# Retention of a two-layer hybrid block: a chunked recurrence in place of the full quadratic form

## The chip, the cores and the metric

The kernel runs on one core of a Trainium2 chip. The metric is the device time of one execution in microseconds. The core has five engines with queues of their own that meet only at semaphores: TensorE (PE), VectorE (DVE), ScalarE (ACT), GpSimd (POOL) and SyncE (SP), which starts the DMA transfers. All data are fp32; the large projections are done in three passes over high and low parts (fp32r).

## The reference

512 latent tokens x and 256 context tokens h, width 1024, pass through two layers. Each layer: a modulated RMSNorm, one input projection to 2304 columns, three head groups (retention, windowed attention, gMLP gating), an output projection, then a SwiGLU FFN. The change is in retention (4 heads of 64):

```python
def retention_scan(q, k, v, log_gamma, s0):          # CHUNK = 128
    ...
    intra = jnp.where(diff >= 0, jnp.exp(lg[:, :, None] * jnp.maximum(diff, 0.0)), 0.0)
    ...
    def step(s, inp):
        qi, ki, vi = inp
        sc = jnp.einsum('bhqd,bhkd->bhqk', qi, ki) * intra
        o = jnp.einsum('bhqk,bhkv->bhqv', sc, vi) + jnp.einsum('bhqd,bhdv->bhqv', qi * q_decay, s)
        s = s * chunk_decay + jnp.einsum('bhkd,bhkv->bhdv', ki * k_decay, vi)
        return s, o
```

It runs forwards and backwards, first over the context from a zero state, then over the latent tokens from the final states of the context. The two outputs are summed, normalised per head and gated:

```python
    o_f, st_f = retention_scan(q, k, v, lg_f, s0_f)
    o_b, st_b = retention_scan(q[:, :, ::-1], k[:, :, ::-1], v[:, :, ::-1], lg_b, s0_b)
    o = (o_f + o_b[:, :, ::-1]).transpose(0, 2, 1, 3)
```

Layer 1 needs no outputs for the context, only its keys and values.

## The kernel before, in words

Activations lie transposed: features on the 128 partitions, tokens along the rows (columns 0 to 511 latent, 512 to 767 context; NT = 768, SX = 512, SC = 256). Chunks 0 to 3 are latent, 4 and 5 context. Every engine has one program written out by hand, in order; a wait holds up all that is behind it on its engine.

A layer runs through these stages:

- Norm, then nine input panels (`in_step`) of two halves. PE does the three passes (L1284 to L1286). ACT makes the high part of the next weights (`hi_a`, L474) and evicts the result; POOL makes the low part (`lo_a`, L379); DVE applies rotary embedding (L965 to L968) to the keys, queries and attention operands. In layer 0, PE also computes the modulation vectors beside the panels: `mod_half` (L1224), whose row DVE copies out (`mod_copy`, L805), and `mod_finish` (L1232), for which PE waits on that copy after the first half of the next panel. At the end of panel 1 in layer 0 DVE computes the logs of the decays (`log_decay_b`, L851 to L865), ahead of the `mod_copy` of that panel.
- gMLP: after the last panel, 48 (layer 0) or 32 (layer 1) small matmul records (L1354).
- Retention, full quadratic form. For each head h and key chunk c there is a job: `score` (L1370) multiplies the 64 features of 128 keys with all 512 queries; DVE multiplies the result with the decay table T or TC (L1038) into Pm; `value` (L1382) multiplies with the values and accumulates over the chunks. There are 24 jobs in each layer, and 8 of 256 columns for context queries in layer 0. PE runs two scores ahead. The tables of a head are made by DVE (L985, L986, L1017, L1018) and ACT (`tables`, L620 to L625). The context's contribution comes through TC, a sum of both directions, without states. The gMLP gates (`gate`, L1002 to L1009) are spread between the jobs on DVE. ACT copies the output to osb (`copy_out`), and PE's attention waits for both halves of it.
- In the same stretch ACT and POOL make the high and low parts of the attention keys and queries (akh, akl, aqh, aql; ACT L474, POOL L436 and L379). Attention waits for the last (qk_lo, 6).
- Attention: scores (L1434 to L1436), softmax (DVE L1092, ACT L704), transposes (L1452), values (L1460), with the group norm of retention in between (L1402, L1408). Then output projection, norm, FFN.

At the start SP loads, in this order: c, constants up to the masks, x, context, five modulation panels, small tensors, three more panels, then the other constants (masks, distances, rotary tables) and the first weights.

Of the kernel before, what the change touches and what calls it, by code (L numbers as in the profile page):

```python
# [21 lines left out]
P = 128  # L22
# [3 lines left out]
SX = 512  # L26
# [30 lines left out]

class Chain:
# [19 lines left out]
def trunk(nc, x, c, ctx_in, c_ctx, w_mod, b_mod, norm1_g, norm2_g, w_in, ret_decay_f, ret_decay_b, ret_norm_g,  # L78
          attn_sink, cm_norm_g, cm_w_s, cm_b_s, w_out, w_gate, w_up, w_down, final_norm_g, consts, out):
    stack = ExitStack()  # L80
    with stack:
# [10 lines left out]
        def overlay(specs, under=()):  # L92
# [10 lines left out]
        K = sb("consts_sb", [P, K_ALL])  # L103
        xT = sb("xT", [P, KC, NT])
        zh = sb("zh", [P, KC, NT], F32R)
# [17 lines left out]
        blg = sb("blg", [P, 16])  # L123
# [3 lines left out]
        eye = K[:, K_EYE:K_EYE + P]  # L127
        ones = K[:, K_ONES:K_ONES + P]
        blk = K[:, K_BLK:K_BLK + P]
        dist = K[:, K_DIST:K_DIST + DIST_W]  # L130
        ropeC = K[:, K_RC:K_RC + SX]
        ropeS = K[:, K_RS:K_RS + SX]
# [28 lines left out]
        T, TC, TD, osb, Pm = overlay([  # L161
            ("T", [P, 2, DIST_W], F32), ("TC", [P, 2, 640], F32), ("TD", [P, 640], F32), ("osb", [P, 2, NT], F32),
            ("Pm", [P, 3, SX], F32)],
            under=[(n + "_r", s, d) for n, s, d in mix_base])

        gn = Pm[:, :, :].rearrange("p a n -> p (a n)").rearrange("p (a n) -> p a n", a=2)
        oc, gsq = gn[:, 0, :], gn[:, 1, :]
# [54 lines left out]
        def _(sp):  # L222
# [7 lines left out]
            sp.dma_start(K[:, 0:K_MASK], consts[:, 0:K_MASK]).then_inc(sem("ld_x"), 16)  # L230
# [24 lines left out]
            sp.dma_start(K[:, K_MASK:K_ALL], consts[:, K_MASK:K_ALL]).then_inc(sem("ld_tables"), 16)  # L255
# [119 lines left out]
        def _(pool):  # L375
# [45 lines left out]
            for l in range(DEPTH):  # L421
# [7 lines left out]

                pool.wait_ge(sem("loA"), 2 * A_OUT[l] + 2)  # L430
# [39 lines left out]
        def _(act):  # L470
# [77 lines left out]
            for l in range(DEPTH):  # L548
# [31 lines left out]
                for p, name in enumerate(PANELS):  # L580
                    for h in range(2):
# [35 lines left out]
                def tables(h):  # L617
                    act.wait_ge(sem(f"T_arg{l}"), h + 1)
                    i, b = l * 4 + h, h % 2
                    nc.scalar.activation(T[:, b, :], T[:, b, :], ACT.Exp)  # L620
                    nc.scalar.activation(TC[:, b, :], dist[:, 0:640], ACT.Exp, bias=blg[:, i:i + 1], scale=lg[:, i:i + 1])
                    if h:

                        act.wait_ge(sem(f"T_done{l}"), h)
                    nc.scalar.activation(TD[:, :], dist[:, 0:640], ACT.Exp, bias=blg[:, 8 + i:9 + i],  # L625
                                         scale=nlg[:, 8 + i:9 + i]).then_inc(sem(f"T_exp{l}"), 1)

                if l == 0:
                    act.wait_ge(sem("ld_tables"), 16)
                tables(0)  # L630
                def copy_out(r):

                    act.wait_ge(sem(f"ret_pv{l}"), (r + 1) * (16 if l == 0 else 12))
                    if l == 0:
                        copy(osb[:, r, SX:NT], ps[:, 6, 0:SC])
                    copy(osb[:, r, 0:SX], ps[:, 5, :]).then_inc(sem(f"osb_rdy{l}"), 1)

                tables(1)
                e = 0
                for c0, c1, s in parts(l == 0):  # L640
                    for r in range(2):
                        act.wait_ge(sem(f"cm_f{l}"), e + 1)
                        copy(zh[:, 6 + r, c0:c1], cmf[:, e % 2, 0:c1 - c0]).then_inc(sem(f"cm_hi{l}"), 1)
                        e += 1
# [153 lines left out]
        def _(dve):  # L798
# [50 lines left out]
            def log_decay_b():  # L849
# [14 lines left out]
                ch.link(V.tensor_scalar(blg[:, 0:8], lg[:, 0:8], float(SX), None, ALU.mult))  # L864
                ch.link(V.tensor_scalar(blg[:, 8:16], lg[:, 8:16], float(SC), None, ALU.mult))  # L865
# [61 lines left out]
            for l in range(DEPTH):  # L927
# [28 lines left out]
                if l == 0:  # L956
                    dve.wait_ge(sem("ld_tables"), 16)
                rope_n = 0
                for p, name in enumerate(PANELS):
                    for h in range(2):  # L960
# [10 lines left out]
                        if l == 0 and p == 1 and h == 1:  # L971
                            log_decay_b()
# [10 lines left out]
                def table(h):  # L983
                    i, b = l * 4 + h, h % 2
                    ch.link(V.tensor_scalar(T[:, b, :], dist, lg[:, i:i + 1], None, ALU.mult))  # L985
                    V.scalar_tensor_tensor(T[:, b, :], dist, nlg[:, 8 + i:9 + i], T[:, b, :], ALU.mult, ALU.min  # L986
                                           ).then_inc(sem(f"T_arg{l}"), 1)

                dve.wait_ge(sem("cm_mm"), l + 1)
                table(0)  # L990
                cm_jobs = [(r, c0, c1, s) for c0, c1, s in parts(l == 0) for r in range(2)]

                def gate(e):

                    if e < len(cm_jobs):
                        r, c0, c1, s = cm_jobs[e]
# [621 lines left out]
```

## Time and profile before

| | |
|---|---|
| median of 3 runs | 2117.64 us (2115.95 to 2118.99) |
| the profiled execution: its own time | 2115.09 us |
| its span, first to last instruction | 2113.3 us |
| mean granted TensorE clock | 0.899 |
| PE, DVE, ACT, POOL busy | 88%, 37%, 25%, 26% |
| retention stage, layer 0 | 279.18 to 394.64 us |
| retention stage, layer 1 | 1421.74 to 1517.91 us |

The page of the profile gives busy times of the engines, the span in 40 slices with the granted clock (PEclk, in tenths of full speed), the chain that ended last, and groups of instructions. A group's row has line, engine, operation, output<-inputs, shapes and count, then busy time and mean ns of one, then the idle time in front and who ended it. A line of the timeline has start, duration, engine, line and operation; "x6" stands for six instructions merged, and the bracket tells how long the engine had been idle and what released it. An fp32 matmul leaves two MATMUL records and two weight loads (PEld); the records of a transpose and of fp32r matmuls are single.

### The profile page before, as it was taken

To read this page: it belongs to the slowest core of one execution; us is meant where nothing else is said; L and a number is where in the kernel's file an instruction comes from. 1 tells how busy PE (TensorE), PEld (TensorE's weight loads), DVE (VectorE), ACT (ScalarE), POOL (GpSimd) and SP (SyncE) were. 2 spreads that over 40 slices of the span, in tenths; PEclk is the share of its full clock that TensorE was granted. 3 is DMA by queue.
4 is the path that set the end of the run, shared out by engine and by line. 5 is a ranking of instruction groups with operands and counts; after the bars stand their busy time and mean duration, and the time that the engine had idled before them with its cause. 6 is when DMAs were issued, how large, how long until landed. Compare 5 with 4: busy or idle time off the path is not lost.

```text
span 2113.3 us, 21910 instructions
## 1 busy us (share of the span) xinstructions
PE 1869.8 (88%) x8746; PEld 1369.4 (65%) x8746; DVE 786.3 (37%) x1194; ACT 537.9 (25%) x850; POOL 550.5 (26%) x244
## 2 busy tenths in 40 slices
PE   4799989787877999999999978879978869999997
PEld 2577732354665888888888867761344647787875
DVE  3331442355245222222222274245253352433335
ACT  3212230245322211111111122332144232222222
POOL 1522211000133322222222213333000344434430
PEclk8799965789987999999999988995689979999999
DMA  6444400000041333332222101230000313132321
GB/s 243 166 139 142 137 20 0 0 1 1 20 139 44 116 100 100 99 99 99 99 99 99 40 21 36 64 80 0 0 1 1 95 44 120 60 119 67 112 79 41
DMA packets 121900, 155.53 MB, mean 74 GB/s; under 512 B 20320, under 2 KB 89712, under 8 KB 121712
## 3 DMA queue, kind: packets, MB, share of 16 engines
q1 hardware_dynamic: 121840, 154.71, 22.7%
q8 instruction: 40, 0.66, 0.1%
q14 instruction: 20, 0.16, 0.0%
HBM read 152.60 MB, written 2.10 MB: 73 GB/s over the span
## 4 chain that ended last, share of the span: by engine, by line
PE 63%; issue 16%; DVE 10%; ACT 5%; POOL 3%; DMA 2%; SPq 1%; POOLq 0%; DVEq 0%; ACTq 0%
PE ps L1284 13%; PE ps L1285 12%; PE ps L1286 12%; PE ps L1510 5%; PE ps L1511 4%; PE ps L1512 4%; PE ps L1382 3%; PE ps L1370 3%; POOL wl L379 2%; PE ps L1224 2%; DVE nxz L920 2%; PE ps L1460 1%; ACT s_at L704 1%; DVE nxz L914 1%; DVE hl L1163 1%
## 5 line engine op out<-in xcount | busy, mean ns | idle before, releaser
L1284 PE MATMUL ps<-zh,wh 128*128 128x512 f32 x1728 | 631.4, 365 | 77.0 <-DVE zl L905 38.1
L379 POOL TENSOR_TENSOR wl<-raw,wh 128x1024 fp32r<-128x1024 f32 x144 | 354.3, 2472 | 1186.2 <-ACT wh L474 1186.2
L1285 PE MATMUL ps<-zl,wh 128*128 128x512 f32 x1728 | 623.4, 361 | 0.0
L1286 PE MATMUL ps<-zh,wl 128*128 128x512 f32 x1728 | 619.5, 359 | 0.0
L1284 PEld LDWEIGHTS ps<-zh,wh 128*128 128x128 f32 x1728 | 333.9, 193 | 173.1 <-issue 70.4
L1286 PEld LDWEIGHTS ps<-zh,wl 128*128 128x128 f32 x1728 | 333.5, 193 | 49.6
L1285 PEld LDWEIGHTS ps<-zl,wh 128*128 128x128 f32 x1728 | 334.7, 194 | 45.6
L474 ACT ACTIVATE wh<-raw 128x1024 fp32r<-128x1024 f32 x144 | 148.5, 1058 | 409.7 <-PE ps L1286 206.4
L1176 DVE SCALAR_TENSOR_TENSOR xT<-ps,modcol,xT 128x512 f32<-128x512 f32 (+1 forms) x264 | 169.3, 661 | 103.2 <-PE ps L1512 99.2
L1157 DVE TENSOR_TENSOR hf<-gs,ps 128x512 f32<-128x512 f32 x66 | 37.5, 596 | 414.3 <-ACT gs L748 414.3
L1510 PE MATMUL ps<-hh,wh_d 128*128 128x512 f32 x480 | 173.1, 361 | 12.2 <-DVE xT L1176 12.2
L1511 PE MATMUL ps<-hl,wh_d 128*128 128x512 f32 x480 | 171.5, 357 | 0.0
L1512 PE MATMUL ps<-hh,wl_d 128*128 128x512 f32 x480 | 170.8, 356 | 0.0
L748 ACT ACTIVATE gs<-ps 128x512 f32<-128x512 f32 x44 | 26.3, 597 | 461.8 <-PE ps L1286 461.8
L379 POOL TENSOR_TENSOR wl_d<-raw_d,wh_d 128x1024 fp32r<-128x1024 f32 x40 | 95.0, 2397 | 174.1 <-ACT wh_d L474 174.1
L1382 PE MATMUL ps<-Pm,vtok 128*64 128x512 f32 (+1 forms) x112 | 102.2, 1023 | 12.3 <-DVE Pm L1038 12.3
L1163 DVE TENSOR_TENSOR hl<-hf,hh 128x768 fp32r<-128x768 f32 (+1 forms) x44 | 76.6, 1742 | 95.3 <-ACT hh L474 95.3
L1510 PEld LDWEIGHTS ps<-hh,wh_d 128*128 128x128 f32 x480 | 91.2, 190 | 30.0 <-DVE xT L1176 16.5
L1370 PE MATMUL ps<-rq,rk 64*128 64x512 f32 (+1 forms) x112 | 102.5, 1020 | 0.0
L1512 PEld LDWEIGHTS ps<-hh,wl_d 128*128 128x128 f32 x480 | 90.8, 189 | 13.5
L1511 PEld LDWEIGHTS ps<-hl,wh_d 128*128 128x128 f32 x480 | 91.2, 190 | 12.7
L474 ACT ACTIVATE wh_d<-raw_d 128x1024 fp32r<-128x1024 f32 x40 | 40.1, 1052 | 212.1 <-PE ps L1512 212.1
(198 smaller groups left out, 1741.6 us busy)
## 6 DMA issues: line engine op xcount, KB each, us to landing
raw<-in_w_gate_dram SPq DMA_DIRECT2D x22, 1024.0 KB, 7.1
raw<-in_w_up_dram SPq DMA_DIRECT2D x22, 1024.0 KB, 9.5
raw_m<-in_w_mod_dram SPq DMA_DIRECT2D x22, 1024.0 KB, 5.1
raw_d<-in_w_down_dram SPq DMA_DIRECT2D x20, 1024.0 KB, 5.1
raw<-in_w_in_dram SPq DMA_DIRECT2D x14, 1024.0 KB, 5.3
raw<-in_w_mod_dram SPq DMA_DIRECT2D x11, 1024.0 KB, 5.2
raw_n<-in_w_mod_dram SPq DMA_DIRECT2D x9, 1024.0 KB, 5.2
raw<-in_w_out_dram SPq DMA_DIRECT2D x32, 256.0 KB, 4.3
```

Source lines behind the costliest of these rows:

```text
L379: nc.gpsimd.tensor_tensor(dst, src, hi.bitcast(F32), ALU.subtract).then_inc(sem(done), 1)
L474: return nc.scalar.activation(dst, src, ACT.Copy)
L1163: V.tensor_tensor(hl[:, par, h, 0:W], hf[:, 0:W], hh[:, par, h, 0:W].bitcast(F32), ALU.subtract).then_inc(sem(f"h_rdy{l}"), 1)
L1176: last = V.scalar_tensor_tensor(xT[:, n, c0:c1], src, modcol[:, 48 * l + 40 + n, sc:sc + 1], xT[:, n, c0:c1], ALU.mult, ALU.add)
L1284: MM(dst, wt_h[:, h, w], zh[:, k, c0:c1], start=(k == 0), stop=False)
L1285: MM(dst, wt_h[:, h, w], zl[:, k, c0:c1], start=False, stop=False)
L1286: last = MM(dst, wt_l[:, h, w], zh[:, k, c0:c1], start=False, stop=(k == KC - 1))
L1370: MM(ps[:, j % 3, 0:q.stop - q.start], rk[b:b + 64, r, P * c:P * c + P], rq[b:b + 64, r, q], start=True, stop=True).then_inc(sem(f"ret_sc{ ...
L1382: last = MM(ps[b:b + 64, 5 + s, 0:n], vtok[:, c, HD * h:HD * h + HD], Pm[:, j % 3, 0:n], start=first, stop=(c == 5))
L1510: MM(dst, wd_h[:, k, w], hh[:, par, k, c0:c1], start=(k == 0), stop=False)
L1511: MM(dst, wd_h[:, k, w], hl[:, par, k, c0:c1], start=False, stop=False)
L1512: last = MM(dst, wd_l[:, k, w], hh[:, par, k, c0:c1], start=False, stop=(k == 1))
```

## The change

Retention becomes a recurrence over chunks of 128 tokens, in both directions. Within a chunk the decayed scores are used as before, with one table of 128x128 a head (`tab[:, 0:4]`). Between chunks there are 64x64 states: keys are transposed to tokens (TR), multiplied with a decay (kfb), multiplied with the values on PE (the sums, written over the transposes in PSUM), and DVE chains them up over F_ORDER and B_ORDER into five states in each direction (`states`). Queries multiplied with a decay (qfb, made on POOL) read the states in `ret_values`, which accumulates on top of the inner part.

Tables and arguments are no longer made in the retention stage: `decay_args` is put on DVE behind the rotary step of panel 1 (ahead of `mod_copy`), its exp on ACT behind panel 2, `decay_end` on DVE behind panel 3. The gates are taken out of the jobs. On ACT the high parts of the attention queries move behind the copies of the output. The constants in SBUF shrink from 3458 to 2688 columns, and their second transfer becomes three. The core of the diff:

```diff
-            sp.dma_start(K[:, K_MASK:K_ALL], consts[:, K_MASK:K_ALL]).then_inc(sem("ld_tables"), 16)
+            for to, of, n in ((S_MASK, K_MASK, 1152), (S_DIST, K_DIST + 384, P), (S_RC, K_RC, 2 * SX)):
+                sp.dma_start(K[:, to:to + n], consts[:, of:of + n]).then_inc(sem("ld_tables"), 16)
...  (POOL, ahead of the attention keys)
+                pool.wait_ge(sem("tab_rdy"), l + 1)
+                pool.wait_ge(sem(f"rope_done{l}"), 5)
+                pool.wait_ge(sem("use_a"), 2 * A_OUT[l])
+                nq = NT // P if l == 0 else SX // P
+                for d in range(2):
+                    for r in range(2):
+                        nc.gpsimd.tensor_tensor(qfb[:, d, r, 0:P * nq]..., rq[:, r, 0:P * nq]...,
+                                                tab[:, 4 + 2 * d + r, :]..., ALU.mult).then_inc(sem("qf_rdy"), 1)
...  (ACT)
+                        if p == 2 and h == 1:
+                            act.wait_ge(sem("tab_arg"), l + 1)
+                            nc.scalar.activation(dcol[:, :], dcol[:, :], ACT.Exp)
+                            nc.scalar.activation(tab[:, :, :], tab[:, :, :], ACT.Exp).then_inc(sem("tab_exp"), 1)
...
+                cm_hi(0)
+                cm_hi(1)
                 act.wait_ge(sem("use_a"), 2 * A_OUT[l])
...
                 for kv in range(2):
                     rows = slice(HD * kv, HD * kv + HD)
                     copy(akh[rows, kv, :], ak[rows, :]).then_inc(sem(f"qk_hi{l}"), 1)
+                copy_out(0, 0)
+                copy_out(1, 0)
+                if l == 0:
+                    cm_hi(2)
+                    cm_hi(3)
+                    copy_out(0, 1)
+                    copy_out(1, 1)
                 for q in range(4):
                     copy(aqh[:, q, 0:W], aq[:, q, 0:W]).then_inc(sem(f"qk_hi{l}"), 1)
-                tables(2)
-                copy_out(0)
-                tables(3)
-                copy_out(1)
...  (DVE: decay_args, 2 linked copies, 5 small scalings, then)
+                for h in range(4):
+                    ch.then(V.tensor_scalar(tab[:, h, :], dist, lg[:, 4 * l + h:4 * l + h + 1], None, ALU.mult))
+                for j in range(4):
+                    ch.then(V.tensor_scalar(tab[:, 4 + j, :], dist, tpos[:, 0:1], None, ALU.add))
+                ch.wait()
...  (4 scalar_tensor_tensor and 4 tensor_scalar of 128x128)
...  (DVE in the retention stage)
+                dve.wait_ge(sem("tab_rdy"), l + 1)
+                for c2 in range(3):
+                    decayed_keys(c2)
+                weigh(0, 0)
+                weigh(1, 0)
                 dve.wait_ge(sem("cm_mm"), l + 1)
+                gate(0)
+                gate(1)
+                states()
+                weigh(2, 0)
+                weigh(3, 0)
+                gate_lo(0)
+                gate_lo(1)
+                if l == 0:
+                    gate(2)
+                    gate(3)
+                    for h in range(4):
+                        weigh(h, 1)
+                    gate_lo(2)
+                    gate_lo(3)
...  (PE)
+                for c2 in range(3):
+                    for c in (2 * c2, 2 * c2 + 1):
+                        for r in range(2):
+                            last = TR(ps[:, c2, at:at + P], rk[:, r, P * c:P * c + P], eye)
+                    last.then_inc(sem("kt_mm"), 1)
+                def ret_scores(r, s):
+                    for i in range((4, 2)[s]):
+                        for q in range(2):
+                            b, h = 64 * q, 2 * r + q
+                            last = MM(ps[...], rk[b:b + 64, r, P * c:P * c + P], rq[b:b + 64, r, P * c:P * c + P], ...)
+                ret_scores(0, 0)
+                pe.wait_ge(sem(f"cm_f{l}"), 2)
+                ret_scores(1, 0)
+                for c2 in range(3):
+                    pe.wait_ge(sem("kt_ev"), 3 * l + c2 + 1)
...  (for c, d, r, q)
+                                    last = MM(ps[64 * q:64 * q + 64, c2, at:at + HD], kfb[:, c, d, HD * h:HD * h + HD],
+                                              vtok[:, c, HD * h:HD * h + HD], start=True, stop=True)
+                pe.wait_ge(sem("st_rdy"), l + 1)
+                if l == 0:
+                    pe.wait_ge(sem("cm_f0"), 4)
+                    ret_scores(0, 1)
+                    ret_scores(1, 1)
+                def ret_values(r, s):
+                    pe.wait_ge(sem("ret_p"), 8 * l + 4 * s + 2 * r + 2)
...  (for c in chunks, q: inner part; then wait for qf_rdy; for d, c, q: state part)
+                            MM(dst(c, q), vtok[:, c, HD * h:HD * h + HD], Pm[:, h, P * c:P * c + P], ...)
+                                last = MM(dst(c, q), St[b:b + 64, slot, d, r, :], qfb[b:b + 64, d, r, P * c:P * c + P], ...)
```

`decayed_keys` is two multiplies of 128x512 from PSUM; `weigh` is the L1038 operation with `tab`; `states` is 4 copies and 4 rounds of 4 multiply-adds, all 128x64, with the sums read from PSUM. PE's new work in layer 0 is 12 transposes, 16 + 8 scores of 128 columns (32 + 16 records), 48 sums of 64 columns (96 records) and 64 values of 128 columns (128 records); in layer 1 it is the same without the context's 8 scores and 16 values.

## Rows read from the trace of the kernel before

**Rows 1.** The page: busy us, share of the span and instructions of each engine.

```profile
PE 1869.8 (88%) x8746; PEld 1369.4 (65%) x8746; DVE 786.3 (37%) x1194; ACT 537.9 (25%) x850; POOL 550.5 (26%) x244
```

**Rows 2.** The page: the group of the values' matmuls, all shapes together.

```profile
L1382 PE MATMUL ps<-Pm,vtok 128*64 128x512 f32 (+1 forms) x112 | 102.2, 1023 | 12.3 <-DVE Pm L1038 12.3
```

**Rows 3.** Timeline of PE: first scores, first attention matmul, in layer 0 and 1.

```profile
279.18 2.84 PE L1370 MATMUL ps<-rq,rk 64*128 64x512 f32 x6
...
394.64 0.38 PE L1434 MATMUL ps<-wh,zh 128*128 128x256 f32 x1 [0.96 <-ACT osb L474]
...
1421.74 0.69 PE L1370 MATMUL ps<-rq,rk 64*128 64x512 f32 x1
...
1517.91 0.38 PE L1434 MATMUL ps<-wh,zh 128*128 128x256 f32 x1 [0.69 <-ACT osb L474]
```

**Rows 4.** Stretch inside layer 0's stage: PE, PEld, DVE, ACT, POOL busy (count), PEclk, DMA.

```profile
300.00:390.00 90.00, 90.00 (x105) 20.43 (x104) 28.27 (x43) 11.34 (x16) 17.66 (x10) 0.50 0.00 0
```

**Rows 5.** PE behind the start wait (timeline), then stretches of PE with granted clock.

```profile
288.85 1.97 PE L1382 MATMUL ps<-Pm,vtok 128*64 128x512 f32 x2 [6.84 <-DVE Pm L1038]
290.75 2.07 PE L1370 MATMUL ps<-rq,rk 64*128 64x512 f32 x2
...
285.00:287.00 2.00, 0.00 (x0) 0.50 0.00 0
394.00:396.00 2.00, 1.36 (x11) 1.00 0.00 0
```

**Rows 6.** gMLP matmuls, layer 0 (timeline, stretches of them alone); old loop's weight loads.

```profile
275.00 4.24 PE L1354 MATMUL ps<-wsT,cvt 128*64 128x128 f32 x48 [0.59 <-ACT rg L608]
...
275.00:276.00 1.00, 1.00 (x10) 0.50 0.00 0
278.00:279.20 1.20, 1.20 (x24) 1.00 (x19) 1.00 1.06 265
...
L1382 PEld LDWEIGHTS ps<-Pm,vtok x112: 178/227/232, 288.9 to 1515.5; 128*64 128x64 f32 x112
```

**Rows 7.** Groups of VectorE by shape, 275 to 400 us, and 119 to 125 us (L857).

```profile
L1038 DVE SCALAR_TENSOR_TENSOR Pm<-ps,T 128x512 f32<-128x512 f32 x16 | 10.8, 688 | 24.6 <-PE ps L1370 23.4 <-issue 1.2
...
L1002 DVE SCALAR_TENSOR_TENSOR rtmp<-ps,vcol,bsb 128x512 f32<-128x512 f32 x2 | 1.5, 742 | 0.0
...
L1017 DVE TENSOR_TENSOR T<-T,consts_sb 128x128 f32<-128x128 f32 x4 | 1.1, 287 | 4.0 <-ACT TD L625 4.0
L1002 DVE SCALAR_TENSOR_TENSOR rtmp<-ps,vcol,bsb 128x256 f32<-128x256 f32 x2 | 0.9, 474 | 0.0
...
L857 DVE TENSOR_TENSOR lt<-lt 128x16 f32<-128x16 f32 x6 | 1.0, 175 | 0.2
```

**Rows 8.** High and low parts of attention's queries (timeline); copy of the output (groups).

```profile
310.10 3.04 ACT L474 ACTIVATE zh<-aq 128x768 fp32r<-128x768 f32 x4
...
320.40 7.09 POOL L379 TENSOR_TENSOR zl<-aq,zh 128x768 fp32r<-128x768 f32 x4
...
1448.46 6.06 POOL L379 TENSOR_TENSOR zl<-aq,zh 128x512 fp32r<-128x512 f32 x4
...
L474 ACT ACTIVATE osb<-ps 128x512 f32<-128x512 f32 x2 | 1.2, 592 | 0.0
```

**Rows 9.** Timeline of ScalarE: the load of exp's function table, layer 0.

```profile
281.24 1.28 ACT L620 ACT_TABLE_LOAD   x1 [6.33 <-DVE T L986]
```

**Rows 10.** Timeline around the log decays (layer 0), then VectorE beside GpSimd in layer 1.

```profile
124.47 2.36 POOL L379 TENSOR_TENSOR wl<-raw,wh 128x1024 fp32r<-128x1024 f32 x1 [7.18 <-ACT wh L474]
...
125.16 1.05 PE L1232 MATMUL ps<-sel,modrow 128*128 128x2 f32 x8 [1.94 <-DVE modrow L805]
...
1324.11 0.01 DVE L965 LOAD_MASK_SELECT shuf<-rtmp  x1 [5.26 <-ACT rtmp L474]
...
1402.19 2.17 DVE L945 TENSOR_SCALAR cmst<-cmst 128x16 f32<-128x16 f32 x1
```

**Rows 11.** Stretch of the start, PE alone: busy (count), PEclk, DMA share, GB/s.

```profile
50.00:60.00 10.00, 5.85 (x32) 0.63 1.03 381
```

More of the change, by code:

```diff
@@ L615, in _, with cm_hi, copy_out @@
                                                  ).then_inc(sem("cm_std"), 1)
[L617 to L644, printed above, removed]
+                def cm_hi(e):
+                    r, c0, c1 = [(r, c0, c1) for c0, c1, s in parts(l == 0) for r in range(2)][e]
+                    act.wait_ge(sem(f"cm_f{l}"), e + 1)
+                    copy(zh[:, 6 + r, c0:c1], cmf[:, e % 2, 0:c1 - c0]).then_inc(sem(f"cm_hi{l}"), 1)
+                def copy_out(r, s):
+                    act.wait_ge(sem("ret_o"), 4 * l + 2 * s + r + 1)
+                    c0, n, bank = (0, SX, 0) if s == 0 else (SX, SC, 5)
+                    copy(osb[0:64, r, c0:c0 + n], ps[0:64, bank + r, 0:n])
+                    last = copy(osb[64:128, r, c0:c0 + n], ps[64:128, bank + 1 - r, 0:n])
+                    if s or l:
+                        last.then_inc(sem(f"osb_rdy{l}"), 1)
+                cm_hi(0)
+                cm_hi(1)
                 act.wait_ge(sem("use_a"), 2 * A_OUT[l])
@@ L1021, in _ @@
[L1021 to L1042 removed]
+                    r, c0, c1, s = cm_jobs[e]
@@ new lines, in grown, with states @@
+                def grown(c, d, r):
+                    at = 256 * (c % 2) + P * d + HD * r
+                    return ps[:, c // 2, at:at + HD]
+                def states():
+                    dve.wait_ge(sem("u_mm"), 3 * l + 3)
+                    for d, order in enumerate((F_ORDER, B_ORDER)):
+                        for r in range(2):
+                            ch.then(V.tensor_copy(St[:, 0, d, r, :], grown(order[0], d, r)))
+                    for i in range(1, 5):
+                        ch.wait()
+                        for d, order in enumerate((F_ORDER, B_ORDER)):
+                            for r in range(2):
+                                last = V.scalar_tensor_tensor(St[:, i, d, r, :], St[:, i - 1, d, r, :],
+                                                              dcol[:, 8 + 2 * d + r:9 + 2 * d + r], grown(order[i], d, r),
+                                                              ALU.mult, ALU.add)
+                                if i < 4 or not (d and r):
+                                    ch.then(last)
+                    last.then_inc(sem("st_rdy"), 1)
@@ new lines, in ret_scores @@
+                def ret_scores(r, s):
+                    for i in range((4, 2)[s]):
+                        c = 4 * s + i
+                        for q in range(2):
+                            b, h = 64 * q, 2 * r + q
+                            at = P * i if s == 0 else SC * r + P * i
+                            last = MM(ps[:, (5, 6, 3, 4)[h] if s == 0 else (7, 2)[q], at:at + P], rk[b:b + 64, r, P * c:P * c + P],
+                                      rq[b:b + 64, r, P * c:P * c + P], start=True, stop=True)
+                    last.then_inc(sem("ret_sc"), 2)
@@ L1392, in _ @@
+                ret_values(0, 0)
+                ret_values(1, 0)
+                if l == 0:
+                    ret_values(0, 1)
+                    ret_values(1, 1)
                 gn_jobs = [(r, c0, c1) for r in range(2) for c0, c1, s in parts(l == 0)]
```

216 lines of the change are left out of this document (118 added, 98 removed).

## The prediction

> **What bounds the kernel now.** The page comes first. TensorE is busy for 88% of the span, VectorE for 37%, ScalarE and GpSimd for a quarter each [rows 1]. The change touches retention alone, so the second view is the groups of matmuls by shape. The two matmuls of the full quadratic form, the score (L1370) and the value (L1382), are 224 records (each fp32 matmul leaves two, 112 in each group) and 205 us of PE's 1870 (102.2 for the value, the score's group alike) [rows 2]. The third view is the stages. From the first score to the first matmul of attention (L1434), layer 0 takes 394.64 - 279.18 = 115.5 us and layer 1 takes 1517.91 - 1421.74 = 96.2 us [rows 3]. Inside, between 300 and 390 us, PE is busy all the time, and no other engine for a third of it [rows 4], so PE sets the time of this stage. But it is PE at a granted clock of 0.50, which is 1.2 GHz: the projections just before it and the attention scores just after it stand at 1.00 [rows 4, 5]. The stage first waits 6.84 us for the decay tables, and the clock falls in that pause [rows 5]. After that a 512-column record takes 0.85 us and goes on doing so, since score and value alternate: one uses 64 rows of the array, the other 64 columns. Whatever makes this stage shorter moves everything behind it forward, since attention waits for the retention output.
>
> **What the change removes.** All 224 records, the eight table rounds on ScalarE and VectorE, and the start wait: the whole 115.5 us and 96.2 us are replaced. The sum therefore follows the new stage as a relay from the end of the gMLP matmuls (time 0 of each layer) to the first attention score, with every hand-off.
>
> **What a small matmul costs.** New records have 64 or 128 columns, where the old ones have 512. Six score records of 512 columns take 2.84 us at 2.4 GHz [rows 3], 0.43 apart; at 1.2 GHz two of them take 2.07 [rows 5], 0.85 apart. So one of 128 takes 0.107 or 0.213, and one of 64 half of that. The only rows of the same kind are those of L1354 (128 columns, 64-column weights, the two halves of the array in turn): 48 records in 4.24 us [rows 6]. The clock is 1.2 GHz in the first half of that stretch and 2.4 GHz behind, and at 2.4 GHz 24 records start in 1.20 us, 0.05 us each [rows 6]. That is half of 0.107: the two column halves run beside each other, and a weight load of 64 columns hides at 0.05 us. The new code alternates halves everywhere (the two heads of a pair), so I take half price: for 128 columns 0.107 us a record at 1.2 GHz and 0.053 at 2.4, for 64 columns 0.053. For the scores the halves are rows of the array, not columns; no row shows that pairing, and its bounds are half and full price. I take half, since L1354 is the nearest row.
>
> Here a rule speaks against the change. L1354's two halves use the same rows and yet start 0.05 us apart, loads included [rows 6]. The Trainium skill ("TensorE: Matmul & The Clock Gate", Part 3, "The mechanism") says that a weight load overlaps a running matmul only when the row groups differ; by that, and by its P/1.2 for a load (53 ns for 64 columns, an estimate from that page), the 464 records on the path would cost some 25 us more. The trace does not bear it out for this shape, but a load there can be as long as 0.227 us in the old loop [rows 6], so it is a rival below.
>
> **Layer 0, step by step.** (a) Four transposes and the hand-off put the first of six decayed-key multiplies at +0.7; they read PSUM, 128x512, as L1038 does in 0.69 us [rows 7]: +4.8. (b) Two weighings of scores at 0.69: +6.2; the first pair's scores and the other transposes lie beside this. (c) Two gMLP gates, (0.74 [rows 7], 0.69 for the multiply behind it, 0.07 between) each: +9.2. PE stands in front of the second pair's scores, which need the banks that the gates free, and the state matmuls, although ready, are queued behind them. The 6 us pause drops the clock to 1.2 GHz, as the pause in this place does now [rows 5]. (d) Scores of the second pair, 16 records: 1.7 + 0.3: +11.2. (e) 96 records of 64 columns for the key-value sums: 5.1 + 0.3: +16.6. (f) The state chain on VectorE: 4 copies and 16 multiply-adds of 128x64. Between 0.17 (128x16) and 0.29 us (128x128) [rows 7], with starts overlapping, 0.2 each, and 0.2 for four waits: +20.8. (g) Layer 0 alone: two weighings, two low parts (0.69), two half-size gates (0.47 [rows 7] and 0.42): 4.6, to +25.4, before PE may write the context scores, 16 records: +27.4. (h) Values: 128 records; the first 4 us at 1.2 GHz hold 37, the other 91 cost 4.8, and changing between 128-row and 64-row matmuls costs 8 x 0.15 = 1.2 (the old loop takes 3.9 us for a score and a value [rows 5] where four records are 3.41): 10.0, +37.4. (i) ScalarE copies the output out: the last three copy pairs and two small high parts queue up from +35.4: 0.6 x 2 [rows 8] + 0.42 x 2 + 0.38 x 4 = 3.6, +39.0. (j) Now something that was hidden is exposed. The high and low parts of the attention queries come behind these copies: the first high part 0.83, then GpSimd's four low parts, 1.8 us each, 7.2 [rows 8]: +47.0. Attention waits for the last of them. In the old order all this was over by 328, with 67 us of matmuls covering it. The decayed queries on GpSimd (four of 128x768, 7.2 us from 275 on) are done long before (h), and the zeroing and low part of the keys, 10.3 us from +10.6, end at about +21, hidden.
>
> Attention starts at +47.0 instead of +115.5: -68.5 us. **Layer 1** has no (g), 96 value records (4.0 + 3.1 + 0.6 = 7.7), copies of 1.2, a high part of 0.55 (0.83 at two thirds of the width) and four low parts of 1.5 [rows 8]: 20.8 + 7.7 + 1.2 + 0.6 + 6.1 = +36.4 instead of +96.2: -59.8 us.
>
> **What is given back.** (k) In either layer the 6 to 8 us wait for GpSimd starts attention at 1.2 GHz. Its first 24 matmuls, of 256 columns, take 0.115 us each at 2.4 GHz and would take 0.21: some 2 us, as a part hides beside VectorE's row maxima. The softmax's exp also needs its function table loaded, which the decay tables had done: 1.28 [rows 9]. 3.3 each, 6.6 (0 to 10). (l) The decay arguments move into the projections. In layer 0 they stand between the log-decay series and the copy of the modulation row, and PE already waits 1.94 us for that copy [rows 10]: there is no cover. They are 7 small operations at 0.17 to 0.2, 12 of 128x128 at 0.2 and 4 at 0.27: 4.8 us. GpSimd's weight split begins at 124.47, and a VectorE operation on 16 columns that meets such a split took 2.17 us instead of 0.17 [rows 10]: +2.0. All 6.8 us are PE waiting (3 to 8). The Trainium skill ("GPSIMD Engine Reference", 1. Specifications) says that the two engines share SBUF interfaces and that VectorE suffers with two SBUF inputs or in a two-port mode; the 2.17 agrees, and without the rule the sum would be 2.0 lower. In layer 1 VectorE is idle for 5.26 us behind this place [rows 10] and hides it. The exps on ScalarE (one load, 1.3, and 1.1) fit in its 7 us gaps. (m) The table transfer falls from 3074 columns (1536 KB) to 2304 (1152 KB), at the 381 GB/s of that stretch [rows 11] 1.0 us earlier for the first weights, which the chain waits for; the two more issues take part of it: -0.5 (-1.0 to 0). (n) The identity add to the tables (128x512) sits where nothing waits: 0.
>
> **The sum.** -68.5 - 59.8 + 6.6 + 6.8 - 0.5 = -115.4 us against the profiled execution's 2115.09 (its span is 2113.3): 1999.7. The median of the three runs, 2117.64, is 2.6 above it: 2002 us.
>
> **Rivals.** *No pairing, low clock.* Each record pays full price and the clock stays at 1.2 GHz, as in the old loop, which never recovered although PE was full. Layer 0: scores 1.7 + 1.7, sums 5.2, values 128 x 0.213 + 1.2 - 10.0 = 18.5, together 27.1; layer 1: 1.7 + 5.2 + 13.3 = 20.2: 2049. For it: half-array matmuls held the clock down; against it: L1354 reached 2.4 GHz within 3 us. *Clock up throughout.* 4.1 + 3.3 us less on the path, 4 less at the start of attention, and the modulation stall at its lower bound, 3.8: 1987. For it: PE rose to 1.00 in L1354; against: the pauses. *Loads in the open: slower.* If each record waits for its own load, 0.227 us, and then moves at 0.213, the 464 records on the path (256 in layer 0, 208 in layer 1) cost 0.44 instead of my mean of 0.071 us: +171, 2173 us, slower than before by 2.6%. It turns slower than before from (115.4 / 464) + 0.071 = 0.32 us a record. For it speaks the skill's rule above, against it that L1354 pays 0.05 to 0.11. *It doesn't do what it says:* if retention were covered by something else, the time would stay; PE full from 300 to 390 and its release of attention speak against it.
>
> **Chances.** My sum 0.67, no pairing 0.14, clock up 0.12, loads in the open 0.04, no change 0.03. The time is that of the sum. The range takes in clock up and reaches two thirds of the way to no pairing: 1985 to 2034. About 0.2% (4 us) is what a measurement of this kernel can tell from no change: faster 0.95, same 0.01, slower 0.04.
>
> **What would show it.** The stretch from the last gMLP matmul to the first attention score should be 47 and 36 us, with PE idle in three gaps: before the second pair's scores, under the state chain, and 6 to 8 us before attention, released there by GpSimd. The value records should start 0.05 to 0.11 us apart in pairs. The modulation-row wait of layer 0 should grow from 1.9 to 8 to 9 us. Projections, output projection and FFN should not move. If records start 0.2 us apart, pairing fails; if VectorE's state chain takes 8 us instead of 4.2, step (f) is the error; a slowdown anywhere outside these places would make the whole account wrong.

## The result and the profile after

The changed kernel takes 1996.81 us (median of 4 runs, 1991.61 to 1997.73) against 2117.49 us: a ratio of 0.9425, 95% interval 0.9407 to 0.9443. The forecast was 2002, range 1985 to 2034. The profiled execution took 1996.34 us, its span is 1994.3 (2113.3 before), its mean granted clock 0.926 (0.899).

The page of the changed kernel, the row that answers to [rows 1]:

```profile
PE 1722.9 (86%) x9042; PEld 1365.6 (68%) x9042; DVE 756.9 (38%) x1220; ACT 524.8 (26%) x837; POOL 559.5 (28%) x252
```

PE is busy for 147 us less, and the span is 119 us shorter: some of the saved work has turned into waiting. The timeline of PE in layer 0's stage, after the change (transposes L1445, scores L1455, sums L1469, inner part L1490, state part L1498, attention L1549):

```profile
281.29 4.43 PE L1434 MATMUL ps<-wsT,cvt 128*64 128x128 f32 x48 [0.59 <-ACT rg L628]
285.66 1.53 PE L1445 MATMUL ps<-consts_sb,rk 128*128 128x128 f32 x12
287.12 1.16 PE L1455 MATMUL ps<-rq,rk 64*128 64x128 f32 x16
294.50 2.08 PE L1455 MATMUL ps<-rq,rk 64*128 64x128 f32 x16 [6.22 <-DVE rtmp L1052]
296.50 3.79 PE L1469 MATMUL ps<-vtok,kfb 128*64 128x64 f32 x96
308.87 2.08 PE L1455 MATMUL ps<-rq,rk 64*128 64x128 f32 x16 [8.58 <-DVE rtmp L1052]
310.88 1.57 PE L1490 MATMUL ps<-Pm,vtok 128*64 128x128 f32 x16
312.38 1.96 PE L1498 MATMUL ps<-qfb,St 64*64 64x128 f32 x32
314.28 1.09 PE L1490 MATMUL ps<-Pm,vtok 128*64 128x128 f32 x16
315.30 1.96 PE L1498 MATMUL ps<-qfb,St 64*64 64x128 f32 x32
...
318.95 0.65 PE L1498 MATMUL ps<-qfb,St 64*64 64x128 f32 x8
329.02 0.55 PE L1549 MATMUL ps<-wh,zh 128*128 128x256 f32 x1 [9.41 <-POOL zl L388]
```

The three waits in brackets are the gaps that the prediction named; the small matmuls between them add up to some 20 us, where the old stage had PE busy nearly throughout. From the end of the gMLP matmuls to attention: 329.02 - 285.66 = 43.4 us instead of 115.5 [rows 3]. VectorE in the same stretch shows who fills the first two gaps:

```profile
286.79 3.68 DVE L1066 TENSOR_TENSOR kfb<-ps,dcol 128x512 f32<-128x512 f32 x6 [5.89 <-PE ps L1445]
290.39 1.28 DVE L1078 SCALAR_TENSOR_TENSOR Pm<-ps,tab 128x512 f32<-128x512 f32 x2
...
293.75 0.69 DVE L1052 TENSOR_TENSOR rtmp<-rtmp,cu 128x512 f32<-128x512 f32 x1
300.34 0.62 DVE L1091 COPY St<-ps 128x64 f32<-128x64 f32 x4 [5.90 <-PE ps L1469]
301.00 3.53 DVE L1096 SCALAR_TENSOR_TENSOR St<-St,dcol,ps 128x64 f32<-128x64 f32 x16
...
305.64 1.38 DVE L1059 TENSOR_TENSOR zl<-rtmp,zh 128x512 fp32r<-128x512 f32 x2
...
308.30 0.43 DVE L1052 TENSOR_TENSOR rtmp<-rtmp,cu 128x256 f32<-128x256 f32 x1
```

The third gap is the relay ScalarE, then GpSimd (their timelines): high parts of the queries, then their low parts. Exp's table load comes beside the low parts.

```profile
320.85 3.04 ACT L494 ACTIVATE zh<-aq 128x768 fp32r<-128x768 f32 x4
323.91 1.28 ACT L720 ACT_TABLE_LOAD   x1
...
321.84 7.08 POOL L388 TENSOR_TENSOR zl<-aq,zh 128x768 fp32r<-128x768 f32 x4 [15.97 <-ACT zh L494]
```

Layer 1, PE's timeline: 1397.42 - 1362.09 = 35.3 us instead of 96.2 [rows 3].

```profile
1362.09 2.05 PE L1445 MATMUL ps<-consts_sb,rk 128*128 128x128 f32 x12
...
1373.02 4.74 PE L1469 MATMUL ps<-vtok,kfb 128*64 128x64 f32 x96
1382.05 1.98 PE L1490 MATMUL ps<-Pm,vtok 128*64 128x128 f32 x16 [4.29 <-DVE St L1096]
...
1397.42 0.55 PE L1549 MATMUL ps<-wh,zh 128*128 128x256 f32 x1 [7.07 <-issue]
```

What was given back stands at the modulation row: VectorE's timeline, then PE's. PE waits 8.44 us where it waited 1.94 [rows 10].

```profile
123.52 2.19 DVE L890 TENSOR_SCALAR lgq<-lgq 128x2 f32<-128x2 f32 x1
...
129.78 0.68 DVE L822 COPY modrow<-ps 128x512 f32<-128x512 f32 x1
...
130.52 1.87 PE L1312 MATMUL ps<-sel,modrow 128*128 128x2 f32 x8 [8.44 <-DVE modrow L822]
```

The whole difference of the spans adds up by stage: gMLP of layer 0 starts 6.3 us later (281.29 against 275.00), layer 0's stage -72.1, layer 1's -60.8, the two gMLP stages +0.5, from attention to the end of the feed-forward +0.7 in layer 0, from attention to the end +1.4 in layer 1, and from the end of layer 0's feed-forward to layer 1's gMLP +5.0: -119.0. Each of these terms carries scatter of some microseconds. In the second profile of the changed kernel (run 8) the stages took 44.9 and 33.6 us instead of 43.4 and 35.3, and the gMLP of layer 0, with the same code ahead of it, started at 275.00 in the kernel before and at 270.60 in run 4.

### The profile page after: what moved, and what is told of

Read it like the earlier page. It is cut to its first block, busy times and chain, and to the rows that moved or that the text cites. A ratio compares the mean times of both kernels' runs of the same rounds, so it can differ in the third digit from the quotient of the medians.

```text
span 1994.3 us, 22475 instructions
## 1 busy us (share of the span) xinstructions
PE 1722.9 (86%) x9042; PEld 1365.6 (68%) x9042; DVE 756.9 (38%) x1220; ACT 524.8 (26%) x837; POOL 559.5 (28%) x252
## 4 chain that ended last, share of the span: by engine, by line
PE 63%; issue 14%; DVE 11%; ACT 5%; POOL 3%; DMA 2%; SPq 2%; POOLq 0%; DVEq 0%; ACTq 0%
PE ps L1364 13%; PE ps L1365 13%; PE ps L1366 13%; PE ps L1625 5%; PE ps L1626 5%; PE ps L1627 5%; PE ps L1304 2%; POOL wl L388 2%; DVE nxz L969 2%; PE ps L1575 1%; ACT s_at L721 1%; DVE nxz L963 1%; DVE hl L1243 1%; POOL zl L388 1%; PE ps L1312 1%
## 5 line engine op out<-in xcount | busy, mean ns | idle before, releaser
L1627 PE MATMUL ps<-hh,wl_d 128*128 128x512 f32 x480 | 170.8, 356 | 0.0
L1575 PE MATMUL ps<-pT,vtok 128*64 128x512 f32 x160 | 85.5, 682 | 0.8 <-ACT pT L494 0.8
L1549 PE MATMUL ps<-wh,zh 128*128 128x256 f32 (+1 forms) x144 | 52.5, 364 | 32.6 <-DVE stats L1172 15.9
```

The costliest lines, as they stand in the source:

```text
L1549: MM(dst, aqh[:, c, blk_q], akh[:, kv, keys], start=True, stop=False)
L1575: last = MM(ps[64 * kv:64 * kv + 64, 7, :], vtok[:, tile, 256 + HD * kv:256 + HD * kv + HD], pT[:, kk, :], start=(kk == 0), stop=(kk == le ...
L1627: last = MM(dst, wd_l[:, k, w], hh[:, par, k, c0:c1], start=False, stop=(k == 1))
```

## The experiments

All are timed against the kernel before on the same chip. One per cent of it is 21 us.

**1. The copy of the modulation row first.** In the changed kernel:

```diff
                             if l == 0:
+                                mod_copy(M_IN + 4)
                                 log_decay_b()
...
-                    if l == 0:
+                    if l == 0 and p != 1:
                         mod_copy(M_IN + 2 * p + 2)
```

> The changed kernel, with the copy of the modulation row of panel 1 (layer 0) put ahead of the log decays and the decay arguments on VectorE; nothing else moves. Theory: PE's 8.4 us wait for that copy is all this chain, the 6.5 us that the change added and the 1.9 us that were there before, so the wait goes below 0.5 us and the kernel takes 1988 us (8 to 9 less than the 1996.8 of the changed kernel). Rival: the projections are bound by something else here (the rotary step's buffers, or the next weights), a new wait of 5 us or more appears within the next panels, and the time stays at 1993 or above.

Measured: 1980.13 us, ratio 0.9354 [0.9329, 0.9379], 15 us under the changed kernel by the ratios. The waits of PE for the row (total, times, longest) go from `15.7, 6, 8.4` in the changed kernel to:

```profile
PE ps L1313 <- DVE modrow L822: 7.3, 5, 4.3
```

That is 8.4 us, and the gMLP of layer 0 starts at 272.58 instead of 281.29. So the wait of 8.4 us was all in the open, as (l) has it, and the old 1.94 too. The wait has a tail that (l) leaves out: behind it the projections run at a granted clock of 0.50 for 7 us. The stretch behind the wait in the changed kernel, then the same matmuls in this kernel (PE busy, PEclk):

```profile
130.50:137.50 7.00, 6.98 (x25) 0.50 0.29 79
```

```profile
124.20:128.20 4.00, 4.00 (x29) 1.00 0.14 23
```

From the row's matmuls (130.52 against 124.25) to the same record of the next panel (137.55 against 127.97) the changed kernel falls back by another 3.3 us. Wait and tail are 11.7 us, and against the profile of run 8, in which layer 1's projections took as long as here, the span is 12.3 us shorter (1977.6 to 1989.9). The 15 us of the medians also hold the scatter of layer 1's projections (run 8).

**2. No pairing.** Scores, sums and values in loops with the head of a pair outermost, so that neighbours use the same half of the array:

```diff
-                    for i in range((4, 2)[s]):
-                        c = 4 * s + i
-                        for q in range(2):
+                    for q in range(2):
+                        for i in range((4, 2)[s]):
+                            c = 4 * s + i
```

> The changed kernel with the same matmuls in another order: scores, sums and values of one head of a pair first, then those of the other, so that neighbours use the same half of the array. Theory (halves in turn run beside each other, for half the price): each record on the path costs twice as much at the same clock. At 2.4 GHz: scores +3.4 and +1.7, sums +1.3 and +1.0, values +5 and +3 us: 2012 us. If single halves also keep the clock at 1.2 GHz, sums are 10.2 us, values 27 and 20 us: 2044 us. Rival (weight loads or a fixed cost per record set the pace, not pairing): the order makes no difference, 1997 us, and starts stay 0.05 us apart.

Measured: 2005.05 us, ratio 0.9477 [0.9447, 0.9507], 11 us over the changed kernel. Its PE timeline in layer 0, to be laid beside the rows above:

```profile
286.18 1.71 PE L1455 MATMUL ps<-rq,rk 64*128 64x128 f32 x16
...
296.59 5.47 PE L1469 MATMUL ps<-vtok,kfb 128*64 128x64 f32 x96
...
318.15 1.58 PE L1490 MATMUL ps<-Pm,vtok 128*64 128x128 f32 x16
319.66 3.32 PE L1498 MATMUL ps<-qfb,St 64*64 64x128 f32 x32
```

Unpaired against paired, at the same clock (1.00; the sums' 5.47 and 3.79 us are not, as more of them fell into the low clock here): 3.32 to 1.96 us for 32 state records (0.104 and 0.061 each), 1.58 to 1.09 for 16 inner ones, 1.71 to 1.16 for 16 scores. So row halves pair too, the open point of the prediction, but pairing gives a factor of 1.45 to 1.7 and not 2. The Trainium skill ("TensorE: Matmul & The Clock Gate", "Why this matters for your kernels") says that small-K matmuls in different row groups run at the same time; the 1.16 agrees for two halves, with a gain of 1.47. The stages grow by 6.6 and 3.1 us. The clock still reached 1.00 in the values: no pairing with a low clock, the rival of 2049, was wrong in both halves.

**3. The state sums ahead of the second pair's scores.**

```diff
-                pe.wait_ge(sem(f"cm_f{l}"), 2)
-                ret_scores(1, 0)
...  (sums)
                     last.then_inc(sem("u_mm"), 1)
+                pe.wait_ge(sem(f"cm_f{l}"), 2)
+                ret_scores(1, 0)
```

> The changed kernel with PE's key-value sums put ahead of its wait for the gMLP gates and the second pair's scores. Theory: the sums are ready while PE waits for the gates, so the state chain on VectorE starts right behind the second gate, 5.8 us earlier in each layer: 1985 us, the gMLP-to-attention stretch 37.6 and 29.5 us instead of 43.4 and 35.3. Rival: the sums only fill the wait, PE falls to 1.2 GHz anyway and the values behind take longer by what was won: a gain under 4 us, 1993 or above.

Measured: 1987.09 us, ratio 0.9379 [0.9352, 0.9407], 10 us under. Layer 1's stage is 27.8 us instead of 35.3 (33.6 in run 8), so there the theory holds; layer 0's is 42.3 instead of 43.4. There the state chain also ended 6.0 us earlier in the stage, at 299.5, and yet the context scores started only 1.9 us earlier (21.3 us into the stage instead of 23.2). VectorE's timeline in this kernel:

```profile
299.45 1.28 DVE L1078 SCALAR_TENSOR_TENSOR Pm<-ps,tab 128x512 f32<-128x512 f32 x2
300.65 3.66 DVE L1059 TENSOR_TENSOR zl<-rtmp,zh 128x512 fp32r<-128x512 f32 x2
304.23 0.47 DVE L1050 SCALAR_TENSOR_TENSOR rtmp<-ps,vcol,bsb 128x256 f32<-128x256 f32 x1
304.74 1.17 DVE L1052 TENSOR_TENSOR rtmp<-rtmp,cu 128x256 f32<-128x256 f32 x1
...
306.34 1.51 DVE L1052 TENSOR_TENSOR rtmp<-rtmp,cu 128x256 f32<-128x256 f32 x1
```

GpSimd works on the keys' parts from 297.00 to 307.58 here. The two low parts take 3.66 instead of 1.38 us and the two half-size multiplies 1.17 and 1.51 instead of 0.42 and 0.43: 4.1 us. In the changed kernel the same operations came at 305.64, as GpSimd ended at 305.87, and met it little. L1050, which reads one operand from PSUM, stays at 0.47. The Trainium skill ("GPSIMD Engine Reference", 1. Specifications) says that VectorE suffers beside GpSimd with two SBUF inputs; these rows agree.

**4. The old kernel, with scores over the full height of the array.** It tests what held the clock at 0.50 for 90 us [rows 4]:

```diff
-... rk[b:b + 64, r, P * c:P * c + P], rq[b:b + 64, r, q], ...
+... rk[:, r, P * c:P * c + P], rq[:, r, q], ...
```

> The kernel before, quadratic form, with each score matmul over all 128 rows instead of the 64 of its head (the scores of the two heads of a pair are added up, so this part of the computation is changed); same records, columns, order and waits. Theory: half-height matmuls kept the old loop at 1.2 GHz; with full rows the granted clock goes to 1.00 some microseconds after the start, a job costs 2 us instead of 3.9 and both stages shrink by 40 to 50 us: 2027 us, so most of the change's gain would be a matter of the clock. Rival (the pause at the start or the alternation of score and value holds the clock down, whatever the rows): the clock stays at 0.50, only the cost of changing between 64 and 128 rows (0.24 us a change, some 13 us) goes: 2104 us.

Measured: 2044.56 us, ratio 0.9664 [0.9635, 0.9693]. The same number of records and columns as before, and 71 us less. Stretches of this kernel (as in [rows 4]), then its PE timeline:

```profile
279.00:290.00 11.00, 5.29 (x8) 1.28 (x8) 7.61 (x12) 5.16 (x7) 0.00 (x0) 0.69 0.00 0
290.00:300.00 10.00, 10.00 (x24) 2.63 (x22) 8.38 (x15) 3.84 (x7) 1.52 (x1) 1.00 0.00 1
300.00:340.00 40.00, 35.95 (x78) 9.43 (x78) 23.27 (x30) 8.26 (x12) 16.23 (x9) 1.00 0.00 0
...
284.71 1.97 PE L1382 MATMUL ps<-Pm,vtok 128*64 128x512 f32 x2 [6.83 <-DVE Pm L1038]
286.61 1.82 PE L1370 MATMUL ps<-rq,rk 128*128 128x512 f32 x2
288.36 1.07 PE L1382 MATMUL ps<-Pm,vtok 128*64 128x512 f32 x2
```

The clock falls in the same start wait (6.83 us; 6.84 in [rows 5]), but is up again from 288.36 on (a record pair takes 1.07 instead of 1.82 to 1.97 us) and stays at 2.4 GHz, where the old loop with half-height scores stayed at 1.2. Layer 0's stage is 72.0 us, 43.5 shorter, where the change brings 72.1; layer 1's is 65.7, 30.5 shorter, where the change brings 60.8. So the low clock alone was worth some 60% and 50% of the gain in the stages (the step from a value to the next score takes 1.90 us at 0.50 in both kernels, whatever the height). It is a measure and not an offer: this kernel does not compute retention, and a quadratic form with full-height scores that does was not tried. In the recurrence the clock came back by itself, perhaps because its half-height stretches are short, which no run separates. That the height of the scores decides in the old loop is shown; whether it is the low height itself or the change between two heights, and why, is not.

**5. The queries' low parts on VectorE.**

```diff
...  (GpSimd: the four are taken out)
+                for q in range(4):
+                    dve.wait_ge(sem(f"qk_hi{l}"), 3 + q)
+                    V.tensor_tensor(aql[:, q, 0:W], aq[:, q, 0:W], aqh[:, q, 0:W].bitcast(F32), ALU.subtract
+                                    ).then_inc(sem(f"aq_lo{l}"), 1)
```

> The changed kernel, with the four low parts of the attention's queries (zl <- aq minus its high part, 128x768 in layer 0) moved from GpSimd to VectorE, behind VectorE's last low part of a gate; everything is computed as before. In the changed kernel the PE waits 9.41 us for the last of these four in layer 0 (GpSimd works on them from 321.84 to 328.92, 1.77 us each) and 7.07 us in layer 1 (4.93 us for the four). Theory (these four stand in the open, and the wait is theirs): ScalarE makes the four high parts in 3.04 us (320.85 to 323.89), VectorE is idle by then and follows each, its nearest row (a 128x512 subtraction of the key's low part) at about 0.6 us for 512 columns gives about 0.8 us for 768, so the first attention score starts about 4 us earlier in layer 0 and 3 us earlier in layer 1: about 1990 us, 7 under the changed kernel. Rival (the wait belongs to ScalarE's chain of output copies and high parts, or the exp table load behind it, and GpSimd only comes last by name): no more than 1 us, 1996. A difference in layer 1's stage between the attention of layer 0 and the second matrix stage, which nothing here touches, would be the clock's phase and not this edit.

Measured: 1990.54 us, ratio 0.9411 [0.9396, 0.9427]. The ratio's interval overlaps that of the changed kernel, so the time alone doesn't settle it; the timelines of VectorE and PE do:

```profile
322.43 3.56 DVE L1121 TENSOR_TENSOR zl<-aq,zh 128x768 fp32r<-128x768 f32 x4 [1.93 <-ACT zh L490]
...
326.25 0.55 PE L1550 MATMUL ps<-wh,zh 128*128 128x256 f32 x1 [5.94 <-DVE zl L1121]
```

PE waits 5.94 instead of 9.41 us in layer 0 and 4.68 instead of 7.07 in layer 1, 3.5 and 2.4 less: the theory, slightly oversized. The stages are 39.9 and 32.7 us long. The rest of the wait is ScalarE's: it can't make the high parts earlier, since the decayed queries (qfb) lie in the same bytes of SBUF as the queries' high parts. A version with another place for them was not tried.

**6. The context scores behind the latents' output** (layer 0).

```diff
-                if l == 0:
-                    pe.wait_ge(sem("cm_f0"), 4)
-                    ret_scores(0, 1)
-                    ret_scores(1, 1)
...  (latents' values)
                 if l == 0:
+                    pe.wait_ge(sem("cm_f0"), 4)
+                    ret_scores(0, 1)
+                    ret_scores(1, 1)
                     ret_values(0, 1)
```

> The changed kernel, with layer 0's context scores (16 matmuls, 308.87 to 310.95) put behind the latents' output matmuls instead of ahead of them; everything is computed as before. In the changed kernel the PE is idle 8.58 us ahead of these scores, waiting for VectorE's gate of the context, while the state copies that the latents' output needs are done at 304.53 at the latest (16 state operations from 301.00, 3.53 us). Theory (the order holds the latents' output back from the end of the state chain to the end of the context gates): the latents' inner and state parts start at about 304.5 instead of 310.88 and their 6.9 us run beside the context's gates, so that the last output comes about 4 to 5 us earlier and the attention too: about 1992 us. Rival (ScalarE's and GpSimd's chain behind the outputs sets the attention's start, since VectorE's low parts of the gates, or the context's scores with their own wait, come last anyway): within 1 us of the changed kernel, 1996. Layer 1 has no context scores and should not move.

Measured: 1989.71 us, ratio 0.94 [0.9383, 0.9416]. PE's timeline:

```profile
303.51 1.58 PE L1486 MATMUL ps<-Pm,vtok 128*64 128x128 f32 x16 [4.29 <-DVE St L1096]
...
310.96 1.16 PE L1455 MATMUL ps<-rq,rk 64*128 64x128 f32 x16
```

The latents' values run where PE had been idle, and the scores behind them wait for nothing. Layer 0's stage is 39.8 us, 3.6 less than in the first profile of the changed kernel and 5.1 less than in run 8's; layer 1's, 34.7, stays within the 33.6 and 35.3 of these two. The interval of the ratio overlaps that of the changed kernel, so here too the timeline decides and not the time.

**7. All four moves together** (1, 3, 5 and 6).

> The changed kernel with four moves at once, all computing the same: the copy of the modulation rows ahead of VectorE's small decay operations in layer 0, the second pair's latent scores behind the state sums, the context scores behind the latents' output, and the queries' low parts on VectorE. The first alone measured 17 us under the changed kernel, the second alone 10 us. Theory (four separate waits; the second lost some 4 us in layer 0 only because the context scores, which the fourth move takes off the path, stood behind gates slowed by GpSimd): 1996.8 less 17, less 10 to 14, less 4, less 7: about 1957 us. Rival (the waits overlap: once one is gone the next chain, ScalarE's copies or VectorE's gates, ends last at nearly the same time, and the phase of the clock gave part of the first move's 17 us and is not given twice): about 1970 us.

Measured: 1960.88 us (1959.53 to 1968.63), ratio 0.9268 [0.9253, 0.9284]: faster than both kernels. By the ratios it is 33 us under the changed kernel, and the four alone add up to 15 + 10 + 3 + 5 = 33. Each of these carries 5 to 7 us of its own, so the match is closer than it can show; it does rule out the rival's 1970 as the median. The stages are 31.2 and 26.1 us. PE's timeline, layer 0:

```profile
274.81 3.45 PE L1468 MATMUL ps<-vtok,kfb 128*64 128x64 f32 x96
281.08 1.77 PE L1456 MATMUL ps<-rq,rk 64*128 64x128 f32 x16 [2.81 <-DVE rtmp L1049]
285.17 1.98 PE L1487 MATMUL ps<-Pm,vtok 128*64 128x128 f32 x16 [2.32 <-DVE St L1093]
...
303.48 0.55 PE L1550 MATMUL ps<-wh,zh 128*128 128x256 f32 x1 [5.54 <-DVE zl L1122]
```

**8. The changed kernel once more.**

> The changed kernel itself, run again beside the three others. It tells whether layer 1's projections, in which nothing was changed, again take about 5 us more than in the kernel before (from the end of layer 0's feed-forward matmuls to the start of layer 1's second matrix stage: 188.1 us before, 193.1 us in the changed kernel, and the granted clock in the records fell at other moments). Theory (the clock's phase follows from the kernel's own sequence and so repeats): 193 us again, and 1997 us in all. Rival (it is a matter of one execution): 188 us, and a time of its own between 1992 and 1997.

Measured: 1992.96 us (1991.22 to 1995.82), ratio 0.9425 [0.9409, 0.9441]. The next three rows run from a point 17 us before the end of layer 0's feed-forward matmuls to layer 1's gMLP, first in the first profile of the changed kernel, then in this one, then before (columns as in [rows 4]):

```profile
1165.60:1358.40 192.80, 155.26 (x702) 127.20 (x701) 94.30 (x131) 56.82 (x77) 57.70 (x25) 0.86 0.17 44
```

```profile
1168.10:1356.20 188.10, 149.93 (x703) 123.03 (x702) 94.15 (x131) 56.80 (x77) 57.89 (x25) 0.89 0.17 45
```

```profile
1230.40:1418.40 188.00, 150.09 (x703) 123.14 (x702) 87.70 (x106) 54.44 (x75) 57.79 (x25) 0.89 0.17 45
```

The same code, the same kernel, 4.7 us apart by the granted clock: between the first two rows nothing differs by more than 0.2 us but the busy time of PE and of its weight loads. The rival was right: it goes by the execution. Counted from the end of the feed-forward, the ten profiles take either 170.8 to 171.3 us (before, this one, runs 1 and 2) or 175.6 to 176.7 (the others, the old kernel with full-height scores among them). It is not a matter of the chip: runs 1 to 4 were on one chip and runs 5 to 8 on another, and both have both lengths.

## Why the prediction was right

The mechanism was as told in the retention stages, and the size came out: -119.0 us of span against a sum of -115.4. That it is only 3.6 off is partly luck. The two stages came out 4.7 us shorter than forecast and what follows them (k) 4.5 us cheaper, and against that stood 5.0 us of scatter in layer 1's projections, for which the sum had no term. By its steps in layer 0, from 285.66:

- (a) to (d): the six multiplies end at +4.8 (+4.8), the weighings at +6.0 (+6.2), the gates at +8.8 (+9.2), the second pair's scores at +10.9 (+11.2). PE did stand in front of these scores with the sums queued behind; run 3 shows what that cost, 10 us.
- (e) The sums end at +14.6 instead of +16.6. This is the term most oversized: 3.8 us for 96 records, not 5.1, as the clock was back at 1.00 at 298.2, in the middle of them; from there a record takes 0.029 us, half price (0.027) and not the 0.053 of the low clock. Layer 1, where it came back later, took 4.7.
- (f) The state chain took 4.2 us, from 300.34 to 304.53, as forecast. (g) took 4.2 for 4.6.
- (h) 8.7 us for 10.0. Full price was right (0.104 us a record against 0.107), half price too low (0.061 and 0.068 against 0.053), and the surcharge of 1.2 for changes of shape and the 4 us of low clock too high; the errors partly cancel. The low clock ended at 311.9, after 1.0 us; in layer 1 it lasted 5.1 us, and the part took 8.3 for 7.7.
- (i) 1.2 us for 1.6. (j) The exposed high and low parts took 8.2 us for 8.0: the wait moved here from under the old matmuls, and GpSimd released attention, as named.
- Together 43.4 for 47.0, and 35.3 for 36.4. In layer 1 the low parts took 4.93 us and not 6.06 [rows 8], with VectorE idle beside them; in the kernel before it was making tables at the same time.
- (k) was wrong in mechanism for its smaller part, 1.3 of the 3.3 us a layer: the exp table load came at 323.91, behind the last high part, and was over at 325.19, 3.8 us before attention. It cost nothing. The cold start cost 1.2 us in layer 0's first 24 matmuls (4.56 against 3.36 us). From attention on, the two layers lost 0.7 and 1.4 us, 2.1 in all instead of 6.6; but the profiles of runs 1 to 8 scatter in these stretches from 850.9 to 855.3 and from 595.4 to 602.1 us (852.7 and 595.4 before), so this sum says little.
- (l) 6.5 us of added wait for 6.8: the small operation that met GpSimd's split took 2.19 instead of 0.17 us, and the series behind it is as counted. This operation (L890) and the one of [rows 10] have a single tensor input, so two SBUF inputs are not the reason there; whether it was the two-port mode, the other condition that the prediction names, no run shows. (l) left out the low clock behind the wait, 3.3 us (run 1). (m) The first projection matmul came 1.1 us earlier, for 0.5; but the same code starts it anywhere from 63.3 to 65.8 us in the profiles (64.80 and 65.13 with the old transfer), so (m) isn't shown.
- "Projections should not move" failed by 5.0 us in the profiled execution. Run 8 shows that this is scatter between executions, so it is no cost of the change; but the prediction's range had no term for it. Without it the difference would have been -124.0; in run 8's profile it is -123.4 (1989.9 against 2113.3).

Of the rivals, clock up throughout (1987) is not settled by the time: the changed kernel's median, 1996.81, lies 5 us below the forecast of 2002 and 10 above this rival, run 8's median, 1992.96, 9 below and 6 above. The clock settles it: it did fall where the prediction put it, and the second pair's scores take 2.08 us where the first take 1.16. No pairing with a low clock fell in run 2. Loads in the open is ruled out: the 96 sums of layer 0, with a weight load each, start 0.04 us apart, and 0.029 at the clock of 1.00, where one load takes 0.138 us. The Trainium skill ("TensorE: Matmul & The Clock Gate", Part 3, "The mechanism") has loads overlap a running matmul only between different row groups in one sentence, and in another also when they go to the background weight buffer. These rows disagree with the first, since L1469's halves are columns over the same 128 rows; whether the second is what happens, no run shows.

## What to carry to other kernels

When a long matmul block becomes many small steps, follow the hand-offs as a relay: of the 43 us that remained, PE computes for some 20, and each wait can be read off ahead from who is queued behind whom. Work that was hidden beneath the long block (high and low parts here) has to be priced again, and independent PE work belongs ahead of the first wait. Look at the granted clock of a full PE first: a loop at 0.50 with PE at 100% can account for half or more of the gain that a better algorithm seems to bring (50% and 60% of the stages here). And price a wait of PE with the low clock behind it: 8.4 us of wait cost 11.7 (run 1).

## What was not expected of the hardware

- Score matmuls on 64 of 128 rows, alternating with full-height ones, kept the granted clock at 0.50 with PE always busy; on all 128 rows it was 1.00, and the kernel 71 us shorter (run 4). In the recurrence, half-height records did run at 1.00 (L1498, 2 us from 315.30).
- Untouched code takes 171 or 176 us by the execution, in one kernel, through where and how often the granted clock falls (run 8).
- Pairing half-array fp32 matmuls gave 1.45 to 1.7 times, for row halves as for column halves (run 2).
- VectorE's two-input operations on SBUF beside GpSimd took 2.7 to 3.5 times as long at 256 and 512 columns (run 3: 3.66 for 1.38, 1.17 and 1.51 for 0.42 and 0.43); with one operand in PSUM 0.47 either way. In the changed kernel one of 2 columns, with one tensor input, took 2.19 us.
